# Two convolution products in halves among the index scores, and the low part of the attention's keys on GpSimd

## The reference

```python
h = rms_norm(x, g_mix)
proj = h @ w_in
(c_b, c_c, c_x, q, k, v, iq, ik, iw, g_a, g_b) = split(proj)
y_a = (c_b * causal_depthwise_conv3(c_c * c_x)) @ w_branch_a      # convolution branch
# sparse attention, 8 heads, keys and values shared by the heads
score = einsum("bth,bths->bts", iw, relu(iq . ik))                # index scores
_, idx = top_k(causal(score), 256)                                # 256 positions for each query
logits = q . k[idx] / 8 + rel_bias[bucket(t - idx)]
attn = softmax(logits) . v[idx]
```

## Time and profile before

| | us |
|---|---|
| median of three runs | 2698.06 |
| lowest, highest | 2696.7, 2699.41 |
| the profiled execution, its own time | 2696.2 |
| its span, first to last instruction | 2694.4 |

### The profile page before, as it was taken

How to read it: one execution, slowest core, us unless ns; L and a number is a source line. 1 busy time by engine, 2 the same in 40 slices (tenths; PEclk the granted TensorE clock), 3 DMA queues, 4 the chain that set the end, 5 groups by cost and what they waited for, 6 DMA issues and landing times.

```text
span 2694.4 us, 31682 instructions
## 1 busy us (share of the span) xinstructions
PE 2528.4 (94%) x12088; PEld 2082.7 (77%) x12088; DVE 1727.6 (64%) x2928; ACT 972.7 (36%) x1717; POOL 588.8 (22%) x412
## 2 busy tenths in 40 slices
PE   5999999888899899999999999999999988998888
PEld 3778888667787678888888877888778766788877
DVE  5499999488424787787644368568676564008933
ACT  4431222477223322222311243233242244228732
POOL 2247422333443000000000120000000144324333
PEclk7999999899999899999999999999999989999999
DMA  4112233100454265654523132332264115232143
GB/s 165 44 40 63 79 101 100 38 1 9 137 186 135 77 208 173 198 177 140 219 95 109 59 106 79 102 107 82 94 257 156 47 55 165 85 102 68 47 146 102
DMA packets 260705, 293.16 MB, mean 109 GB/s; under 512 B 10856, under 2 KB 216140, under 8 KB 260556
## 3 DMA queue, kind: packets, MB, share of 16 engines
q1 hardware_dynamic: 260556, 291.14, 33.5%
HBM read 223.95 MB, written 66.10 MB: 108 GB/s over the span
## 4 chain that ended last, share of the span: by engine, by line
PE 63%; DVE 28%; ACT 5%; DMA 1%; issue 1%; POOL 1%; SPq 0%; DVEq 0%; ACTq 0%; POOLq 0%
PE ps L67 62%; DVE sm L100 6%; DVE m L97 6%; DVE tmp L103 2%; DVE tmp L79 2%; DVE sm L79 1%; ACT tmp L73 1%; DVE ptl L79 1%; PE ps L70 1%; DVE tmp L76 1%; DVE p2l L76 1%; ACT pth L73 1%; DVE wl L76 1%; DVE X L79 1%; DVE pwa L76 1%
## 5 line engine op out<-in xcount | busy, mean ns | idle before, releaser
L76 POOL TENSOR_TENSOR wl<-raw,wh 128x512 fp32r<-128x512 f32 (+1 forms) x224 | 293.2, 1330 | 1623.6 <-ACT wh L73 1623.5
L73 ACT ACTIVATE wh<-raw 128x512 fp32r<-128x512 f32 (+1 forms) x388 | 226.4, 621 | 257.5 <-PE ps L67 184.7
L73 ACT ACTIVATE tmp<-ps 128x512 f32<-128x512 f32 (+5 forms) x172 | 127.3, 751 | 391.3 <-PE ps L67 379.9
L67 PE MATMUL ps<-B2h,wh 128*128 128x512 f32 x616 | 245.3, 398 | 12.9 <-DVE B2l L76 6.7
L67 PE MATMUL ps<-B2l,wh 128*128 128x512 f32 x616 | 242.5, 394 | 0.0
L67 PE MATMUL ps<-B2h,wl 128*128 128x512 f32 x616 | 242.4, 393 | 0.0
L76 DVE TENSOR_TENSOR tmp<-tmp,ps 128x512 f32<-128x512 f32 x204 | 138.3, 684 | 108.5 <-PE ps L67 92.6
L67 PE MATMUL ps<-ah,wh 128*128 128x512 f32 (+1 forms) x608 | 191.8, 392 | 14.2 <-DVE xt L85 10.2
L73 ACT ACTIVATE wh<-ws 128x512 fp32r<-128x512 f32 x152 | 94.4, 627 | 289.0 <-DVE ws L76 261.9
L67 PE MATMUL ps<-B3h,wh 128*128 128x512 f32 x448 | 178.3, 398 | 15.2 <-DVE B3l L76 7.0
L67 PE MATMUL ps<-al,wh 128*128 128x512 f32 (+1 forms) x608 | 190.4, 390 | 0.0
(11 more groups left out here) (281 smaller groups left out, 5806.8 us busy)
## 6 DMA issues: line engine op xcount, KB each, us to landing
ada<-in_ada_w SPq DMA_DIRECT2D x48, 512.0 KB, 3.9
raw<-in_w_in SPq DMA_DIRECT2D x37, 512.0 KB, 4.4
raw<-in_a_w_in SPq DMA_DIRECT2D x33, 512.0 KB, 4.6
gates<-tmp SPq DMA_DIRECT2D x32, 512.0 KB, 3.0
raw<-in_w_ffn_gate SPq DMA_DIRECT2D x24, 512.0 KB, 6.4
hd<-tmp SPq DMA_DIRECT2D x22, 512.0 KB, 4.5
gf<-hd SPq DMA_DIRECT2D x22, 512.0 KB, 7.2
raw<-in_a_w_out SPq DMA_DIRECT2D x20, 512.0 KB, 3.5
```

The source lines that it names most:

```text
L67: return self.e.matmul(*a, **k) if self.e else Ins()
L73: return self.e.activation(*a, **k) if self.e else Ins()
L76: return self.e.tensor_tensor(*a, **k) if self.e else Ins()
```

## The change

- **Scores.** `set_apart` takes one of the four PSUM tiles out of the pool for the length of the scores. Before blocks 4, 5, 6 and 7 TensorE does one half (512 columns, 24 matmuls) of a convolution product in it: the two halves of cc of group 0, then the two of cx. ScalarE copies the finished product out between heads 3 and 4 of blocks 5 and 7, into two tiles of their own (`conv0`), and rounds the next weights there; it rounds one more pair of blocks ahead of the first relu. GpSimd makes the matching low parts, the first at the head of the stage, the next behind block 5's cut.
- **Convolution.** Group 0 keeps only cb in `pe_conv` and `act_conv`; the numbers of the `tmp` buffers behind it move by two.
- **Keys.** SyncE copies the keys to both halves of `kt2` with two DMAs; ScalarE rounds all 128 rows in one operation, and the low part is one operation too. For the index it stays on VectorE, for the attention it is GpSimd's, behind the weights of `kv` and ahead of those of the first query product.

```diff
         self.T1 = m("t1", 34, cols=2048)
+        self.conv0 = {"cc": m("cc0", 25), "cx": m("cx0", 27)}
         self.LA = [self.tmp[(self.AT + i) % 5] for i in range(5)] + [m("la5", 25), m("la6", 27)]
...
+    def set_apart(self):
...
+        i = min(self.pool4, key=lambda i: max(h.taken for h in self.halves[2 * i:2 * i + 2]))
+        self.pool4.remove(i)
+        self.apart = i
...
+    def take_apart(self, e, key):
...
+        i = self.apart
+        self.takes += 1
+        for half in self.halves[2 * i:2 * i + 2]:
+            for before in half.before:
+                e.wait_ge(*self.at("free", before))
+            half.before, half.taken = [key], self.takes
+        self.places[key] = self.mem["ps"][i][:, :]
+        self.opened.add((key, "open"))
...
             e.wait_ge(*self.at(*event))
+        e.dma_start(self.kt2[0:64, :], self.kt[0:64, :]).then_inc(self.sig["swap0"].up(("first", 0)), 16)
         e.dma_start(self.kt2[64:128, :], self.kt[0:64, :]).then_inc(self.sig["swap0"].up(("swap", 0)), 16)
...
-        e.wait_ge(*self.at("kt%d" % i))
         for event in after:
             e.wait_ge(*self.at(*event))
-        e.activation(self.KH[0:64, :], self.kt[0:64, :], ACT.Copy).then_inc(self.sig["ahi"].up(("khi", i, 0)), 1)
         e.wait_ge(*self.at("swap", i))
-        e.activation(self.KH[64:128, :], self.kt2[64:128, :], ACT.Copy).then_inc(self.sig["ahi"].up(("khi", i, 1)), 1)
...
-    def dve_k_lo(self, e, i):
-        e.wait_ge(*self.at("khi", i, 0))
-        e.tensor_tensor(self.KL[0:64, :], self.kt[0:64, :], self.KH[0:64, :].bitcast(F32), ALU.subtract).then_inc(
-            self.sig["vlo"].up(("klo", i, 0)), 1)
-        e.wait_ge(*self.at("khi", i, 1))
-        e.tensor_tensor(self.KL[64:128, :], self.kt2[64:128, :], self.KH[64:128, :].bitcast(F32), ALU.subtract).then_inc(
-            self.sig["vlo"].up(("klo", i, 1)), 1)
+        e.activation(self.KH[:, :], self.kt2[:, :], ACT.Copy).then_inc(self.sig["ahi"].up(("khi", i)), 1)
...
+    def k_lo(self, e, i, signal):
+        e.wait_ge(*self.at("khi", i))
+        e.tensor_tensor(self.KL[:, :], self.kt2[:, :], self.KH[:, :].bitcast(F32), ALU.subtract).then_inc(
+            signal.up(("klo", i)), 1)
...
             e.wait_ge(*self.at(*event))
-        self.dve_k_lo(e, 0)
+        self.k_lo(e, 0, self.sig["vlo"])
         e.wait_ge(*self.at("prod", "iw"))
...
+        W, h = self.A["w_in"][0], self.by_norm(self.n1, self.ah, self.al, (0, 1))
+        self.set_apart()
+        us = {}
+        between = {3: ("cc", C_C, 0), 4: ("cc", C_C, 1), 5: ("cx", C_X, 0), 6: ("cx", C_X, 1)}
         for b in range(2, NT):
+            if b - 1 in between:
+                name, c0, half = between[b - 1]
+                if half == 0:
+                    us[name] = self.unit((name, 0), self.w8(W, c0))
+                    self.take_apart(e, (name, 0))
+                self.gemm(e, (name, 0), us[name], h, (half,), end=half == 1)
             for j in range(4):
-                for event in (("iqh", j), ("iql", j), ("klo", 0, 0), ("klo", 0, 1)):
+                for event in (("iqh", j), ("iql", j), ("klo", 0)):
                     e.wait_ge(*self.at(*event))
                 self.pe_logits(e, [("score", b, 2 * j), ("score", b, 2 * j + 1)], self.qh[j], self.ql[j], b)
+        self.pool4.append(self.apart)
...
     def act_scores(self, e):
+        self.act_w(e, ("cc", 0))
         for b in range(2, NT):
...
             for hd in range(8):
+                if b in (5, 7) and hd == 4:
+                    name = {5: "cc", 7: "cx"}[b]
+                    e.wait_ge(*self.at("prod", (name, 0)))
+                    e.activation(self.conv0[name][:, :], self.ps((name, 0))[:, :], ACT.Copy).then_inc(
+                        self.sig["evac"].up(("copy", (name, 0)), ("free", (name, 0))), 1)
+                    self.act_w(e, {5: ("cx", 0), 7: ("cb", 0)}[b])
                 i = (b - 2) * 8 + hd
...
         gps = self.sig["gps"]
+        self.pool_w(e, ("cc", 0))
         for event in self.norm1_over():
...
-    CV, GT, QT, AT, CH, BR = 48, 64, 80, 84, 148, 152
+            if b == 5:
+                self.pool_w(e, ("cx", 0))
...
+    CV, GT, QT, AT, CH, BR = 48, 62, 78, 82, 146, 150
...
+    def conv_at(self, j, n):
...
+        return self.CV + 4 * j + n - 2
...
         for j in range(4):
-            for name, c0 in (("cc", C_C), ("cx", C_X), ("cb", C_B)):
+            for name, c0 in (("cc", C_C), ("cx", C_X), ("cb", C_B))[2 if j == 0 else 0:]:
                 u = self.unit((name, j), self.w8(W, c0 + 128 * j))
...
             e.wait_ge(*self.at("conv", j))
-            i = self.CV + 4 * j + 2
+            i = self.conv_at(j, 2)
             e.dma_start(self.cv[j * 128:j * 128 + 128, :], self.tmp[i % 5][:, :]).then_inc(
...
         for j in range(4):
-            for n, name in ((0, "cc"), (1, "cx"), (3, "cb")):
+            for n, name in ((0, "cc"), (1, "cx"), (3, "cb"))[2 if j == 0 else 0:]:
                 self.act_w(e, (name, j))
-                self.act_copy(e, (name, j), self.CV + 4 * j + n)
+                self.act_copy(e, (name, j), self.conv_at(j, n))
...
         for j in range(4):
-            i = self.CV + 4 * j
+            i = self.conv_at(j, 0)
             x1, x2, y, x3 = (self.tmp[(i + n) % 5] for n in range(4))
+            if j == 0:
+                x1, x2 = self.conv0["cc"], self.conv0["cx"]
             w = [self.vec[:, V_CONV + 4 * k + j:V_CONV + 4 * k + j + 1] for k in range(3)]
...
                 e.wait_ge(*self.at("tap", j, sh))
-                marks = [("y", j, sh)] + ([("tfree", i), ("tfree", i + 1)] if sh == 2 else [])
+                marks = [("y", j, sh)] + ([("tfree", i), ("tfree", i + 1)] if sh == 2 and j else [])
                 e.tensor_tensor(y[:, sh:S], y[:, sh:S], x2[:, 0:S - sh], ALU.add).then_inc(gps.up(*marks), 1)
...
         e.wait_ge(*self.at("kt1"))
-        e.wait_ge(*self.at("klo", 0, 1))
+        e.wait_ge(*self.at("klo", 0))
+        e.dma_start(self.kt2[0:64, :], self.kt[0:64, :]).then_inc(self.sig["swap1"].up(("first", 1)), 16)
         e.dma_start(self.kt2[64:128, :], self.kt[0:64, :]).then_inc(self.sig["swap1"].up(("swap", 1)), 16)
...
                 e.wait_ge(*self.at("gst"))
-                e.wait_ge(*self.at("klo", 1, 1))
+                e.wait_ge(*self.at("klo", 1))
                 self.sp_table(e, "t1", self.T1, 0)
...
         e.wait_ge(*self.at("prod", "kv"))
-        e.wait_ge(*self.at("klo", 0, 0))
+        e.wait_ge(*self.at("swap", 0))
         e.wait_ge(*self.at("prod", "iw"))
...
     def dve_qkv(self, e):
-        self.dve_k_lo(e, 1)
         for j in range(4):
...
         self.pool_w(e, "kv")
+        self.k_lo(e, 1, self.sig["plo"])
         for j in range(4):
...
                 return
-            for event in (("qhi", hd // 2), ("qlo", hd // 2), ("klo", 1, 0), ("klo", 1, 1)):
+            for event in (("qhi", hd // 2), ("qlo", hd // 2), ("klo", 1)):
                 e.wait_ge(*self.at(*event))
```

## The result

The changed kernel took 2704.14 us, the median of eight runs (2701.91 to 2707.62), beside 2698.94 (2696.12 to 2702.85) for the kernel before. The medians are 5.2 us apart. The ratio on record is 1.0027, with a 95% interval of 1.0018 to 1.0037; taken on 2698.94 that is 7.3 us slower, between 4.9 and 10.0. The forecast was 2699.5, with "no difference" as the likeliest outcome. The time lies inside the range of 2692 to 2707, but the change is slower, by about the 5.4 us that were called distinguishable.

What follows compares the result with a forecast made beforehand. The prediction took TensorE to set the start of attention, with holes of 10.6 us in the scores and 2.4 us at the bias table. Its terms, 3.3 + 2.4 - 4.3 = +1.4 us on 2698.06, gave 2699.5, range 2692 to 2707.

Steps and rivals of the forecast that it cites:

- Term 3: Bias table before attention: its load leaves the path, 7.34 us become 3.03, -4.3 us (-2.4 if the clock is low).
- Slack of VectorE and GpSimd: Behind the scores: VectorE, 20 to 22 us later, may be 32 late; GpSimd's third weights have 0.6 us cover; cost nothing.
- The walk of the prediction: Pair-by-pair reckoning of TensorE's score stage with three tiles: ends at 174.9, at most 175.2, against 171.9 before.
- Term 1: Score stage: with one PSUM tile missing, TensorE and ScalarE alternate and the holes are remade; +3.3 us, bounds +1.0 to +5.2.
- The handover between engines: Score pairs: waits from a pair's last issue to its relu and back, 0.25 + 0.06 us, together 0.31 a cycle.
- The copies: Blocks 5 and 7: ScalarE's 2.2 us of copy and weight rounding queue later relus behind them, adding 1.5 and 1.4 us.
- The contention: Head of the score stage: GpSimd rounding weight halves slows VectorE's score operations, 1.5 us, between 0 and 2.5.
- Term 2: Score stage: standstills of 2.65 and 2.8 us in blocks 5 and 7 each bring a 1.2 GHz stretch; +2.4 us, 0 to +6.
- the slower rival: Score stage: waits before every pair lower the clock, two half products run wholly at 1.2 GHz; +9.9 us, 2708; 13%.
- The sum: Whole kernel: 3.3 + 2.4 - 4.3 = +1.4 us on the base of 2698.06, giving 2699.5.
- Faster: the missing tile doesn't bite: Score stage: ScalarE keeps ahead in bursts and TensorE fills its holes, 11.6 us earlier, -15.9 with the table, 2682; 10%.

Runs made afterwards that it cites:

- keys_only: The kernel before with only the keys' part of the change (two DMAs, one rounding, attention's low part on GpSimd): 2.2 us faster than the kernel before.
- spread: The changed kernel with its products cut into 16 steps of six matmuls, ScalarE's copies and weight rounding moved: 2684.5 us, 11.6 us faster than the kernel before.
- copies_moved: The changed kernel with ScalarE's copies ahead of the block's first relu, weights at block 6's head and behind the scores: 9.4 us slower than the kernel before.
- tile_only: The kernel before with one PSUM tile unused in the scores and no products moved: 19.4 us slower than the kernel before.
- half4: The changed kernel with no tile set apart, each half product in a pooled half tile, copies and weight rounding moved: 12.1 us faster than the kernel before.
- tile_fill: tile_only with four unread matmuls more ahead of each pair of blocks 4 to 7: 2.2 us slower than the kernel before.

## Why the prediction came near, and which of its terms were off

**Term 3, the table: right.** Forecast -4.3, measured 7.34 - 3.03 = 4.31, in the changed kernel and in keys_only. The keys of the attention in the tile's view of the changed kernel:

```profile
L76 POOL TENSOR_TENSOR kp<-kt,kp x1: 2406/2406/2406, 483.3 to 483.3; 128x1024 fp32r<-128x1024 f32 x1
```

2.4 us on GpSimd, as put. TensorE came to the table 10.9 us later than in the earlier trace rows and found it loaded.

**Slack of VectorE and GpSimd: right in its verdict.** VectorE was 27.6 us late, not 20 to 22, and 15.15 us of idle time were left. GpSimd's third weights came at 202.80, for products due at 182.73 + 21.8 = 204.5; both sides slid together and no wait shows.

**The score stage, part by part.** The walk of the prediction beside the trace of the changed kernel, both from the first matmul of the scores. A half counts from its first matmul to the next score matmul. The last column is what the low clock cost: the time of the same work at 1.2 GHz less its time at 2.4 GHz elsewhere in the stage (a pair's cycle 3.07 against 2.14, a half 6.27 and 6.85 against 5.68).

| part | walk, us | trace, us | of it the clock |
|---|---|---|---|
| blocks 2 and 3 | 8.85 | 8.62 | 0 |
| four halves | 21.8 | 5.68 + 6.27 + 6.85 + 5.67 = 24.47 | 1.8 |
| pairs of block 4 | 6.5 | 9.45 | 1.9 |
| pairs of block 5 | 9.1 | 9.62 | 0.4 |
| pairs of block 6 | 8.6 | 9.24 | 0 |
| pairs of block 7 | 10.9 | 11.09 | 0 |
| all | 65.7 | 72.49 | 4.1 |

Three of the rows behind it:

```profile
118.86 0.50 PE L67 MATMUL ps<-ah,wh 128*128 128x512 f32 x1
...
164.54 0.73 PE L67 MATMUL ps<-kp,qh 64*128 64x512 f32 x4 [1.10 <-ACT tmp L73]
...
165.97 0.50 PE L67 MATMUL ps<-ah,wh 128*128 128x512 f32 x1
```

The forecast 3.3 is the walk's 65.7 and its allowance of 0.3, less the 62.64 of before. The 9.85 us that the stage lost are about 5.8 of term 1 and 4.1 of term 2.

**Term 1, three tiles: mechanism right, size wrong** (+3.3 forecast, +1.0 to +5.2 as bounds; 5.8 measured). "They are remade by the missing tile" is what the trace shows, pair by pair. Three sizes were off.
- The handover between engines, 0.31 us a cycle. It was read behind a pair that ran without a wait, and its first time, 125.72, is the next pair's first matmul, not the last of the pair. The cycles traced at the full clock are 2.14, 2.31, 2.60 and 2.87 us in blocks 4 to 7, where 1.86, 2.16, 2.45 and 2.71 were put: 0.28, 0.15, 0.15 and 0.16 more, at three cycles a block 2.2 us. Some 0.1 of each is the pair itself: its first four matmuls take 0.53 to 0.57 us to the next ones after a wait, and 0.46 in the middle of a pair.
- The change over between score pairs and products, which the prediction put at nothing. A half takes 5.68 us at the full clock where 24 matmuls were put at 5.45, and the pair ahead of it takes 0.22 more than put (164.54 to 165.97 is 1.43, where 1.21 was). That is 0.45 us for each half, 1.8 in all, and the same 0.5 us that spread shows for each of its steps.
- The copies, put too high. They held the fourth pair back by 1.04 us in block 5 and 0.91 in block 7, where 1.5 and 1.4 were put: 0.95 us less. The contention was also put too high, at 1.5 us on VectorE: the first seven score operations took 5.80 us against 4.96 in the kernel before, and blocks 2 and 3 ended 0.2 us earlier than in the walk. The Trainium skill (GPSIMD Engine Reference, Key points) names this contention, GpSimd against VectorE instructions with two SBUF inputs; the trace agrees, with one operation at 1.45 us against 0.62.

**Term 2, the clock: mechanism wrong, size too small** (+2.4 forecast, 4.1 measured). Two steps failed. "Each should be followed by a stretch at 1.2 GHz" is wrong: the two standstills came (2.04 and 2.12 us, put at 2.65 and 2.8), the first was followed by a fall and the second wasn't, and in block 4 and in copies_moved the clock fell after waits of about 1 us. And a stretch was priced at half of 3.4 us, because the one at the table was so short; the first one here lasted 6.5 us, and tile_only's 45. The kernel before had one as long in the scores (clock 0.84, 0.50 and 0.52 in the three windows from 117 to 126 us), behind waits of 1.75 and 1.59 us, and the prediction put it into the walk but drew no price from it. A row of TensorE and a window of the kernel before:

```profile
119.93 1.22 PE L67 MATMUL ps<-kp,qh 64*128 64x512 f32 x4 [1.59 <-ACT tmp L73]
```

```profile
120.00:123.00 3.00, 3.00 (x18) 2.67 (x20) 2.58 (x5) 2.26 (x4) 0.00 (x0) 0.50 0.00 0
```

The argument against the slower rival, that TensorE at 1.90 of 3.00 us had kept 2.4 GHz, was no argument: tile_only holds the same share at 1.2. That rival had 13%. The Trainium skill (TensorE: Matmul & The Clock Gate, "A second HAM failure mode") describes a kernel that cycles through PSUM, with short idle times between groups of matmuls, and a clock that swings between its two levels. The changed kernel agrees, with two slow stretches in 72.49 us; in tile_only the clock didn't swing but stayed at 0.50 from 122 to 166 us.

**The rest.** 9.85 us of the stage less the 4.3 of the table are the +5.5 up to attention. The sum, +1.4, erred by 4.1 us, some 2.5 of it in term 1 and 1.7 in term 2. Both erred the same way. That the time still lies in the range is owed to term 3 and to the width of the range.

**The rivals.** "Faster: the missing tile doesn't bite" fell: in blocks 4 to 7 twelve of the sixteen pairs wait for ScalarE. Its premise, that the holes can be filled, was true, though: half4 fills them with the same products and four tiles. "Slower by the clock" came true in part and in another place: two of the four halves began at 1.2 GHz, with three and six of their 24 matmuls, and lost 1.8 us, not 10.9; the pairs ahead of them were slow too.

**What stays open.** Why the clock fell at 128.8 us and not at 181; no kernel here tells it. And the part behind the start of attention: the same operations take between 2174.2 us (tile_fill) and 2184.0 us (copies_moved) in the profiled executions. 3.6 us of the 10.1 by which the two spans differ lie there (2180.9 against 2177.3). Much of that may be the execution and not the kernel: the profiled one of the change took 2706.64 us, 2.5 above its median, and where the mean granted clock of the whole is lower this part is longer in most (0.975 and 2174.2 in tile_fill, 0.973 and 2177.3 before, 0.971 and 2180.9 with the change, 0.970 and 2184.0 in copies_moved). Whether the change has a part in it wasn't tested; 5.2 us between the medians leave nothing for it, the ratio with 4.9 to 10.0 leaves room for some 4 us.

## What to carry to other kernels

Before a PSUM tile is taken from a loop between two engines, count the cycle with what is left, by handovers read behind a wait, and allow for TensorE's clock falling in the rhythm that results; here 10.6 us of holes became 17. Price each change between two kinds of matmuls as well. The holes can be filled all the same: the two products made the stage 9.9 us longer than the same work before when they had a tile of their own, 9.4 us shorter when they shared the tiles (half4), and 6.6 us shorter in small steps before every pair (spread, 56.06 against 62.64). And price the parts of a change together where one makes late what the other takes off the path: the keys' move is worth some 4 us alone and some 19 with the late scores.

## What was not expected of the hardware

- TensorE's clock stayed at 1.2 GHz for some 45 us in a loop in which it was busy for 1.90 to 2.93 of 3 us in the windows shown and never waited for more than 1.7 us (tile_only); four matmuls more ahead of each pair kept it at 2.4 GHz and made the stage 12.9 us shorter.
- The same busy share, 1.90 of 3.00 us, stood at clock 1.00 in the kernel before and at 0.50 in tile_only and copies_moved.
- The same standstill of 3.00 us at the start of attention was followed by clock 0.50 in six profiled executions, by 1.00 in two, and by a fall within the next microsecond in two.
- Going from score pairs of 64 rows to product matmuls of 128 rows and back costs 0.29 + 0.21 us (spread), and 0.45 us around a half in the changed kernel.
